# Two routing heads of each layer routed for both token tiles from one weight load, with the expert picks taken in twos

## What is computed

```python
q = einsum('bsd,de->bse', h, w_q).reshape(b, s, 8, 2, 128)
scores = einsum('bshid,hikd->bshik', q, sub_keys)      # 128 keys in each of two halves
top_s, top_i = top_k(scores, 16)
cand = top_s[..., 0, :, None] + top_s[..., 1, None, :] # 256 pairs
best_s, best_j = top_k(cand, 16)
experts = i1 * 128 + i2 ; gates = softmax(best_s)
act = gelu(einsum('td,tkd->tk', h, u_tab[experts]))
out = einsum('tk,tkd->td', gates * act, v_tab[experts])
```

## Time and profile before

| what | value |
|---|---|
| the runs shown, median | 1546.36 us |
| the profiled execution's own time | 1547.98 us |
| its span, first to last instruction | 1546.1 us |
| mean granted TensorE clock | 0.826 of full |
| PE busy (matmul) | 1049.1 us, 68% |
| VectorE (DVE) busy | 1083.2 us, 70% |
| ScalarE (ACT) busy | 575.1 us, 37% |
| GpSimd (POOL) busy | 619.7 us, 40% |
| moved by DMA | 623.55 MB, mean 403 GB/s |

### The profile page before, as it was taken

How to read it: one execution, slowest core, us unless ns; L and a number is a source line. 1 busy time by engine, 2 the same in 40 slices (tenths; PEclk the granted TensorE clock), 3 DMA queues, 4 the chain that set the end, 5 groups by cost and what they waited for, 6 DMA issues and landing times. The chain is left out here.

```text
span 1546.1 us, 19439 instructions
## 1 busy us (share of the span) xinstructions
PE 1049.1 (68%) x6790; PEld 532.8 (34%) x6790; DVE 1083.2 (70%) x2485; ACT 575.1 (37%) x1768; POOL 619.7 (40%) x571
## 2 busy tenths in 40 slices
PE   8898656785854668776775667788588465565555
PEld 6685312333531334332552334333255111111111
DVE  8777998646999685654789767564579965444444
ACT  5544433623444433441544431354234432221222
POOL 0034345442753533443343433444243354455441
PEclk9999877887986988787897788889698777667767
DMA  9289999999999999999999999999999999999997
GB/s 381 89 326 421 420 421 420 421 421 405 422 421 368 411 422 421 421 421 421 409 421 421 421 421 421 421 422 420 422 386 421 421 421 422 421 421 422 421 421 304
DMA packets 86642, 623.55 MB, mean 403 GB/s; under 512 B 10000, under 2 KB 10128, under 8 KB 11792
## 3 DMA queue, kind: packets, MB, share of 16 engines
q0 software_dynamic: 73728, 536.90, 83.7%
q1 hardware_dynamic: 12816, 85.41, 13.4%
HBM read 621.23 MB, written 1.05 MB: 402 GB/s over the span
## 5 line engine op out<-in xcount | busy, mean ns | idle before, releaser
L583 POOL DMA_INDIRECT slots<-experts,idx x512 | 593.2, 1159 | 886.5 <-PE psum L1830 709.9
L1427 DVE CUSTOM_DVE_ANT_0 slots<-slots,h 128x1024 f32<-128x1024 f32 x512 | 615.9, 1225 | 390.8 <-DMA slots<-experts,idx 387.6
L1830 PE MATMUL psum<-slots,diag 64*64 64x512 f32 x4088 | 599.3, 737 | 312.4 <-ACT diag L947 312.3
L1830 PEld LDWEIGHTS psum<-slots,diag 64*64 64x64 f32 x4088 | 175.8, 165 | 684.2 <-ACT diag L947 368.9
L931 ACT ACTIVATE ge<-ge 128x4 f32<-128x4 f32 x130 | 26.7, 205 | 437.3 <-DVE ge L1427 436.3
L1752 PE MATMUL psum<-hT,ring 128*128 128x128 f32 x992 | 131.3, 297 | 20.7 <-DMA ring<-weights 16.0
L931 ACT ACT_TABLE_LOAD x55 | 70.6, 1283 | 194.7 <-DVE ge L1427 194.3
L947 ACT ACTIVATE diag<-cst,ge 128x64 f32<-128x64 f32 x511 | 136.5, 336 | 6.7 <-PE psum L1830 2.5
L1752 PEld LDWEIGHTS psum<-hT,ring 128*128 128x128 f32 x992 | 127.7, 212 | 23.5 <-issue 17.7
L938 ACT ACTIVATE ge<-ge,gate 128x1 f32<-128x1 f32 x512 | 109.1, 283 | 4.2
L1525 PE MATMUL psum<-ring,hT 128*128 128x256 f32 x192 | 52.2, 433 | 17.5 <-DVE work L981 17.5
(11 more groups left out here) (292 smaller groups left out, 1075.4 us busy)
## 6 DMA issues: line engine op xcount, KB each, us to landing
ring<-weights SPq DMA_DIRECT2D x32, 1152.0 KB, 10.0
ring<-weights SPq DMA_DIRECT2D x26, 1024.0 KB, 9.2
slots<-weights SPq DMA_DIRECT2D x11, 1024.0 KB, 20.0
slots<-experts,idx POOLq DMA_INDIRECT x512, 20.8
ring<-weights SPq DMA_DIRECT2D x2, 1056.0 KB
sml<-small SPq DMA_DIRECT2D x2, 652.0 KB, 9.1
slots<-weights SPq DMA_DIRECT2D x1, 1056.0 KB, 9.0
xs<-x SPq DMA_DIRECT2D x2, 512.0 KB, 13.2
```

The costliest lines, as they stand in the source:

```text
L583: pool.indirect_dma_start(out=slot[:, place(E), :], out_offset=None, in_=src, in_offset=bass.IndirectOffsetOnAxis(ap=idx[:, n % 2, e:e + 1 ...
L1427: ins = dve.tensor_tensor_reduce(u, u, h2[:, n % 2, :], 1.0, 0.0, ALU.mult, ALU.add, d[:, i:i + 1])
L1830: ins = pe.matmul(acc[HALF * half:HALF * half + HALF, i, :], diag[rows, d % DIAGS, :], slot[rows, place(E), D + half * 512:D + half * 512 ...
```

## The change

It does five things.

1. **Shared heads.** Heads seven and eight (numbers 6 and 7, `SHARED`) of the two tiles of a layer are routed side by side: tile n's head 6, then tile n+1's head 6, then the same for head 7, n being the even step. The block of weights is loaded once (`owner`, `RING`) and given back after the second tile's use (`given_back`). The odd tile's transposed activations have their own place for that (`hR_`: `W[0]`).
2. **Groups of two picks.** GRP = 2, so 64 groups in a step.
3. **Rows in two densities.** In steps 0 and 2 the rows up to `h2T` of the next tile are spread over the first EARLY = 38 of 64 groups, and the ten routing rows (four of the pair, six of the next tile's own heads) over the other 26. In step 1, 22 mixing rows and six routing rows are spread over all 64. Routing heads are counted by their turn in the order (`turn_of`), not by 8n + h.
4. **`adds`.** Ahead of twelve kinds of rows (`FOLLOWS`) TensorE adds the group that is waiting before it starts on the row.
5. **The opening.** In `MIX0`, `qkv3` and `qkn0` come before `scan0`, the second subtraction of `scan0` becomes `scan_im` behind `qkn1`, `mul1` to `mul3` come later, tile 1's `p`, `qkv0` and `qkv1` come before `route1`. SP loads the first block of `qkv` before the constants.

The diff, cut to its core:

```diff
-GRP = 4
+GRP = 2
@@ rows
-       ... ("h2T", "rp"), ("route0",))
+       ... ("h2T",))
 MIX0
-        "power4", "qkv0", "f", "prep", "fx", "ln", "mul0", "mul1", "mul2", "mul3", "rotate0", "rotate1", "cum", "cm",
-        "qkv1", "rotate2", "bu", "qkv2", "scan0", "qkv3", "qkn0", "scan1", "qkn1", "qkv4", "pool", "qkT", "pre0", "pre1",
-        "mixp", "sq1", "scan2", "scan3", "scan4", "scan5", "scan6", "logits0", "scan7", "big0", "logits1", "scan8",
...
-        ("xT", 1), ("hTe", 1), "rp1", ("u", 1), "soft0", ("uT", 1), "route1", "soft1", ("p", 1), ("up", 1), ("f", 1),
+        "power4", "qkv0", "f", "prep", "fx", "ln", "mul0", "rotate0", "rotate1", "cum", "cm", "mul1", "mul2",
+        "qkv1", "rotate2", "bu", "qkv2", "qkv3", "qkn0", "scan0", "qkn1", "scan_im", "qkv4", "pool", "qkT", "pre0", "pre1",
+        "mixp", "mul3", "sq1", "scan1", "scan2", "scan3", "scan4", "scan5", "scan6", "logits0", "scan7", "big0", "logits1",
...
+        "route0", ("xT", 1), ("hTe", 1), "rp1", ("u", 1), "soft0", ("uT", 1), ("p", 1), ("up", 1), ("qkv0", 1),
+        ("f", 1), ("fx", 1), ("ln", 1), ("qkv1", 1), "route1", "rp2", "soft1", ("cum", 1), ("cm", 1), ("qkv2", 1), ...
+SHARED = (6, 7)
+OWN = tuple(h for h in range(PH) if h not in SHARED)
+EARLY = (TOPK * SHARED[0] - SLOTS - 7) // GRP
+FOLLOWS = {"normT", "u", "qkv0", "y", "glu", "qkT", "att1", "att2", "att3", "att4", "out0", "h2T"}
+def routing(heads):
+    rows = []
+    for (n, h), ahead in zip(heads, heads[1:] + [None]):
+        rows.append((n, (f"route{h}",) + ((("rp%d" % ahead[1], ahead[0]),) if ahead else ())))
+    return rows
+def rows_of(n):
+    if n == STEPS - 1:
+        return [], 0, QUADS
+    pair = [(n + i, h) for h in SHARED for i in range(2)]
+    if n == 0:
+        rows = [(1, r) for r in ((), ("qkn",), ("qkT", "v"))]
+        rows += routing([(0, h) for h in OWN[2:]]) + [(1, r) for r in MIX1]
+    else:
+        rows = [(n + 1, r) for r in MIX]
+    if n % TILES:
+        rows = last_row(rows, n + 1, OWN[0]) + routing([(n + 1, h) for h in OWN])
+        return rows, len(rows), QUADS
+    rows = last_row(rows, n, SHARED[0])
+    late = routing(pair + [(n + 1, h) for h in OWN])
+    ...
+    return rows + late, len(rows), EARLY
@@ script
-            while at < len(rows) * (quad + 1) // QUADS:
+            due = (early * (quad + 1) // until if quad < until else
+                   early + (len(rows) - early) * (quad + 1 - until) // (QUADS - until))
+            while at < due:
                 step, row = rows[at]
+                if FOLLOWS.intersection(row):
+                    order.append(("mix", "adds", n))
@@ ring
+def owner(n, i):
+    return (n - n % TILES, i) if i - CH_ROUTE in SHARED else (n, i)
-RING = [c for c in USES if not in_slot(*c)]
+RING = list(dict.fromkeys(owner(*c) for c in USES if not in_slot(*c)))
+def given_back(n, i):
+    return uses(n + 1, i) if i - CH_ROUTE in SHARED else uses(n, i)
-                    sp.wait_ge(S["chunk_used"], uses(*RING[c - 2]))
+                    sp.wait_ge(S["chunk_used"], given_back(*RING[c - 2]))
@@ SP, the opening
             chunk(CH_POOL)
+            chunk(CH_Q)
             sp.dma_start(cst[:, P:], consts[:, P:]).then_inc(S["cst_in"], 16)
...
-            for i in range(6):
+            for i in range(1, 6):
@@ the odd tile's activations
+        def hR_(n):
+            return W[0][:, :].rearrange("p (a b) -> p a b", a=KD) if n % TILES else hT
@@ VectorE, scan
                     link(tt(w3[0], w3[0], spare, ALU.add))
-                    link(tt(w3[1], w3[1], w3[3], ALU.subtract))
+                if part == 9:
+                    scan_im(n)
@@ TensorE
+            def adds(n):
+                add_last()
```

More of the change, by code:

```diff
@@ L103, with last_row @@
         ("att3", "max3", "nrm3"), ("att4", "attg", "sq"), ("merge", "out0"), ("out1", "x1a"),
[2 rows of a table removed]
-ROUTES = tuple((f"route{h}",) for h in range(1, PH))
+        ("out2", "x1p"), ("out3", "x1"), ("h2T",))
+SHARED = (6, 7)
[7 more added lines that the diff above has]
+    return rows
+def last_row(rows, n, h):
+    step, row = rows[-1]
+    return rows[:-1] + [(step, row + ((f"rp{h}", n),))]
+def rows_of(n):
[12 more added lines that the diff above has]
+    late = routing(pair + [(n + 1, h) for h in OWN])
+    if n == 0:
+        late = [(step, row + ((f"tab{5 + i - 4}", TILES),) if 4 <= i < 7 else row) for i, (step, row) in enumerate(late)]
+    return rows + late, len(rows), EARLY
 def script():
@@ L116, in script @@
     for n in range(STEPS):
-        if n == 0:
-            rows = [(1, r) for r in ((), ("qkn",), ("qkT", "v"))]
-            rows += [(0, r) for r in ROUTES[1:]] + [(1, r) for r in MIX1]
-        else:
-            rows = [(n + 1, r) for r in MIX + ROUTES] if n + 1 < STEPS else []
+        rows, early, until = rows_of(n)
         at = 0
@@ L128, in script @@
             done = at
-            while at < len(rows) * (quad + 1) // QUADS:
+            due = (early * (quad + 1) // until if quad < until else
+                   early + (len(rows) - early) * (quad + 1 - until) // (QUADS - until))
+            while at < due:
                 step, row = rows[at]
-                order += [("mix", s, 2 if s[:3] == "tab" else step) for s in row]
+                if FOLLOWS.intersection(row):
+                    order.append(("mix", "adds", n))
+                order += [("mix", s, step) if type(s) is str else ("mix",) + s for s in row]
                 at += 1
@@ L136, in script @@
                 order += [("mix", "soft" + s[5:], step) for s in row if s[:5] == "route"]
-    for quad in (QUADS, QUADS + 1):
-        order += [("open", n, quad), ("close", n, quad)]
-    return order + [("mix", "drain", STEPS - 1)]
+    return order + [("open", n, QUADS), ("close", n, QUADS), ("mix", "drain", STEPS - 1)]
 ORDER = script()
@@ L158, in chunk_order, with turn_of, routes_before @@
     return order
+def owner(n, i):
+    return (n - n % TILES, i) if i - CH_ROUTE in SHARED else (n, i)
 USES = chunk_order()
-RING = [c for c in USES if not in_slot(*c)]
+RING = list(dict.fromkeys(owner(*c) for c in USES if not in_slot(*c)))
+RSEQ = [(b, int(a[5:])) for kind, a, b in ORDER if kind == "mix" and a[:5] == "route"]
+def turn_of(n, h):
+    return RSEQ.index((n, h))
+def routes_before(stage):
+    return sum(1 for kind, a, b in ORDER[:ORDER.index(stage)] if kind == "mix" and a[:5] == "route")
+def given_back(n, i):
+    return uses(n + 1, i) if i - CH_ROUTE in SHARED else uses(n, i)
 FREE = CH_POOL
@@ L191, in experts_of @@
     start, end = PICKS * n + GRP * quad, PICKS * n + GRP * quad + GRP
-    if start >= PICKS * STEPS:
-        alone = PICKS * STEPS - 2 + quad - QUADS
-        return range(alone, alone + 1)
-    return range(start, min(end, PICKS * STEPS - 2))
+    last = PICKS * STEPS - 1
+    return range(start, min(end, last)) if start <= last else range(last, last + 1)
 BY_VECTOR = {PICKS * STEPS - 1}
@@ L1838, in close @@
                 waiting.append((n, quad))
-            run(dict(warm=warm, pre=pre, logits=logits0, turn=turn0, pv=pv0, normT=normT, xT=normT, u=u, p=p_, f=f_, oua=out_a, bu=bu, qkv=qkv, y=y_, glu=glu, qkT=qkT, att=att, pool=pool_,
+            run(dict(adds=adds, warm=warm, pre=pre, logits=logits0, turn=turn0, pv=pv0, normT=normT, xT=normT, u=u, p=p_, f=f_, oua=out_a, bu=bu, qkv=qkv, y=y_, glu=glu, qkT=qkT, att=att, pool=pool_,
                      mixp=mixp, merge=merge, out=out_b, h2T=h2T, rp=rp, route=route), lambda n, quad: None, close)
```

58 lines of the change are left out of this document (28 added, 30 removed), and 15 rows, old and new, of tables (MIX, MIX0, MIX1).

## The result

The change makes the kernel slower: 1570.25 us in the median of four runs (1568.42 to 1576.19) against 1545.98 us for the kernel before in runs beside them, a ratio of 1.0158 with a 95% interval of 1.0145 to 1.0171. The prediction was 1525.0 us, 1519 to 1536, with 94% on faster. It was wrong in sign.

The account below looks back on a forecast made before the run. The prediction took DMA bytes at 421 GB/s, plus holes when queues ran empty, as the bound. Its terms, -11.2 - 1.9 - 5.2 - 4.8 + 1.5 + 0.5 = -21.1 us, gave 1525 us as a median, range 1519 to 1536.

Parts of the forecast that it names:

- Part 1: Routing loads of heads 6 and 7: one load for two tiles, four loads or 4.72 MB fewer, -11.2 us.
- Part 2: The opening: the new order brings the first logits 1.97 us earlier, -1.9 us, bounds -2.0 to 0.
- Part 3, "`adds` puts the waiting group ahead of that wait": Around `x1`, `h2T` and `rp`: GpSimd's 20 us pauses fall apart into about 8 and 10 us, -4.8 us.
- Part 3, "With groups of two, two picks fewer wait, 5 us of transfer more in reserve": All steps: slots are held for two picks fewer, giving the DMA queue 5 us more transfer in reserve.
- the turn from step 0 to 1: Routing rows at the end of step 0: no group has two rows any more, -5.2 us, bounds -5.7 to 0.
- What is denser: Step 0's picks 12 to 38: VectorE falls 9.5 us behind, mostly covered by the reserve; +1.5 us, 0 to +7.
- step 2's mixing rows: 22 rows in 76 picks, 3.45 per row instead of 4.27; VectorE and TensorE stay under nine tenths busy: zero.
- More instructions: All steps: 126 more gelus, 26 us on ScalarE, covered by its wait for dots: zero.
- Part 4: The end: TensorE's shorter bursts may run the last picks at a lower clock, +0.5 us.
- signs of being wrong: A new dip around 150 to 230 or after 860 us, long TensorE waits for ring loads, or first gather at 86 us.
- sign of being right: GpSimd's longest pause on adds under 15 us; others included 28 loads and no 20 us stretch below about 400 GB/s.
- Rival C: Mixing rows of steps 0 and 2: the engines set the rows' pitch, 72 us longer, 1597 us; chance 0.03.

Follow-up runs that it names:

- experiment 7: The kernel of experiment 1 with the four shared blocks loaded once for each tile again, the order kept: 1547.96 us.
- experiment 11: The kernel before on groups of two, with TensorE keeping one more group waiting ahead of a group with a routing row, all 32 loads: 1546.96 us.
- experiment 1: The kernel after without `adds` ahead of any row, all else kept: 1539.77 us.
- experiment 8: The kernel after with `adds` left out ahead of the four attention steps and `out0`, kept elsewhere: 1545.31 us.
- experiment 9: The kernel after with `adds` placed behind its row's own steps instead of ahead of them: 1541.4 us.
- experiment 6: The kernel of experiment 1 with TensorE keeping one more group waiting ahead of a group with a routing row, added behind the row: 1534.04 us.
- experiment 4: The kernel before on groups of two, with its own order and all 32 loads: 1550.52 us.
- experiment 2: The kernel after on groups of four instead of two, `adds` kept: 1554.66 us.

## Why the prediction was wrong

- **Part 1 (the loads, -11.2 us)** was right in mechanism and bytes. 28 loads and 80.69 MB are there. The price is 8.2 us where the late rows have holes (experiment 7). With most of those closed it wasn't measured alone: the 12.9 us of experiment 11 hold the rest of the order as well.
- **Part 2 (the opening, -1.9 us)** was mis-sized. The multiply did move the logits, whose maximum starts at 45.98 us instead of 48.01. But the prediction said that VectorE is the engine that others wait for up to about 62 us and gave the whole advance to the first indices. Of the advance 1.59 us were left at the operation of the first two lines, before and after. Then a new wait of 1.16 us for TensorE, which the kernel before didn't have, took 1.13 us of it; the wait of 2.72 us for ScalarE stood there before as well. The first gather of the kernel after starts at 85.81 us, 0.45 us earlier than in the earlier trace rows:

```profile
62.11 1.28 DVE L978 SCALAR_TENSOR_TENSOR xs<-psum,rn,xs 128x1024 f32<-128x1024 f32 x1
60.52 1.28 DVE L1038 SCALAR_TENSOR_TENSOR xs<-psum,rn,xs 128x1024 f32<-128x1024 f32 x1
62.97 0.74 DVE L1235 SCALAR_TENSOR_TENSOR ring<-uT,sml,psum 128x128 f32<-128x128 f32 x2 [1.16 <-PE psum L1604]
66.43 0.43 DVE L1038 SCALAR_TENSOR_TENSOR work<-ring 128x256 f32<-128x256 f32 x1 [2.72 <-ACT ring L802]
```

```profile
85.81 1.12 POOL L644 DMA_INDIRECT slots<-experts,idx  x1 [68.26 <-DVE idx L1038]
```

- **Part 3, "`adds` puts the waiting group ahead of that wait" (-4.8 us), is the step that failed.** It costed an operation that is put ahead of another by the one place where that helps (ahead of `h2T`, where TensorE stood idle), and not by the eleven other rows where it is written. There TensorE's order is: sums, then what VectorE waits for; and the sums need weights that ScalarE has not made yet. The prediction never asked who is queued behind the sums. Experiments 1, 8 and 9 give it 30.5 us, 24.9 of them in five rows, and all but 1.6 (1541.4 - 1539.77, within the spread of the runs) by its place ahead of the row.
- **Part 3, "With groups of two, two picks fewer wait, 5 us of transfer more in reserve",** left out that VectorE's cover for a wait is the dots of a group, four of 1.225 us before, two now. In the late routing rows each row asks for scores that stand behind new sums: no such wait with fours, 21 waits with twos (experiment 1), of 1.7 us in the mean and up to 3.0. The prediction's 14.6 us of VectorE for such a row, against 15.2 of DMA, is 16.3 with the mean wait and 17.6 with the longest. So the turn from step 0 to 1 (-5.2 us) did not come: 480 to 500 us lost 3.0 us and 500 to 520 lost 1.9. Experiment 6 removes the wait, and with it the holes from 400 to 520 us. The gain of the smaller group itself is real in the changed order (23.2 us without `adds`) and absent in the old one (experiment 4).
- **The sum itself** hid an interaction. `adds` costs 30.5 us with twos and gains 8.3 us with fours (1562.92 without, 1554.66 with), 38.7 us between the two. By the holes, the attention rows lose alike in both; with fours the late rows have no wait of their own and `adds` repairs long pauses, with twos it takes away the reserve that the late rows need. That last link is read from the places of the holes (experiments 1, 2, 8), not tested by itself.
- **"What is denser" (+1.5 us)** was near for twos: 200 to 220 us lost 3.3 us with `adds` and nothing without. That is partly luck. The prediction has VectorE fall 2.5 us behind in these rows before the change; its own sum, redone for 40 picks, gives 102.5 us of VectorE against 110.8 of DMA, so no lag, and the step to 9.5 us behind was larger than it took it to be. With fours the same stretch lost 7.1 and 11.6 us (200 to 240). The attention rows of step 0 have no term at all in the prediction, and lost 12.6 us. For step 2's mixing rows it wrote zero because both engines would be under nine tenths busy; they lost about 1 us with twos (880 to 1140 us), but 5.9 us with fours and `adds` and 15.9 with fours alone. Busy shares say nothing of a ring in which each engine waits for the next.
- **A pause not costed.** The tables on GpSimd stood at the routing rows before and cost nothing; now the queue is short there. Their part is 2.1 us without `adds`, within the noise; with it the hole there is 10.6 us, of which their part wasn't measured.
- **More instructions (zero)** held nearly. There are 127 gelus more, 25 us of ScalarE. Twos on the old order cost 0.2%, 3.7 us (experiment 4), but the routing matmul first takes 3.6 of them away again with no instruction fewer (experiment 11).
- **Part 4 (the end, +0.5 us)** did not come: from the start of the last dot to the end of the span it is 7.4 us in both profiled executions (1538.72 to 1546.1, 1560.95 to 1568.4).
- **The signs.** Three of the signs of being wrong came: a stretch far below 400 GB/s, a new dip in step 0's dense rows (200 to 220 us), and a first gather at 86 us. One sign of being right came too, GpSimd's longest pause on the sums under 15 us (10.6), and misled: that 15 us cost nothing was read where the queue is full.

Rival C was nearest in kind: rows paced by the chain of the engines. It was to decide from half a microsecond too long per row on; in the attention rows it was 3.9 us (13.84 against 9.96). But it made the chain too long by the density of the rows, and with twos it is `adds` that does: in experiment 9 the same rows, as dense, came every 9.36 us. It was given 3% and 1597 us, since it was priced over all rows, and argued away by VectorE's idle time between 870 and 1110 us in the kernel before, whose order had no `adds`.

## What to carry to other kernels

Before an operation is moved ahead of another in an in-order queue, write down three names: what it waits for, who is queued behind it, and who waits for that one. It may stand ahead only where its input is ready before the next one's. And when a group is made smaller, count what cover it gives each wait and not only the buffers it frees: a wait for scores that four dots hid showed 21 times under two, up to 3 us long.

The version that beats both is that of experiment 6: the shared loads and groups of two, no `adds`, and one more group of sums held back before a routing row, 1534.04 us, 0.8% less than the kernel before (ratio 0.9916 [0.9900, 0.9933]).

## What the runs showed of the hardware

- **TensorE's clock makes the wait worse.** In the kernel after the sums that follow an idle of 3.61 us ran in part at the lower clock: 32 matmuls in 6.42 us, and the stretch has a granted clock of 0.82. In experiment 9, with shorter idles between, the same stretch had a clock of 1.00, and 16 took 1.95 us, so 3.9 for 32. Of the 13.84 us of a row some 2.5 are this. The Trainium skill, page "TensorE: Matmul & The Clock Gate", section What's actually happening, has the clock fall to 1.2 GHz for an array that idles; the trace agrees: 16 matmuls took 3.69 us after an idle of 15.33 us (experiment 1) and 1.95 us after one of 1.73 us (experiment 9), which is nearly the ratio of the two levels.
- **VectorE and GpSimd are slow at the same time.** While GpSimd made tables in the kernel after, VectorE's dots took 1.29 to 1.47 us where their mean is 1.226, and pairs of 128x128 operations of GpSimd took 2.61 to 2.83 us, whereas pairs of twice that width took 1.19 to 1.39 us some 12 us later, with the same line, and pairs of 128x128 took 0.77 to 1.64 us in the kernel before. One of VectorE's index operations, 0.17 us in the median of 31, took 3.09 us at 403.58 us, beside the wide pairs. That they hinder each other is the likely reading and wasn't tested alone. Two of the dots, and the index operation:

```profile
385.50 1.29 DVE L1491 CUSTOM_DVE_ANT_0 slots<-slots,h 128x1024 f32<-128x1024 f32 x1
...
392.10 1.47 DVE L1491 CUSTOM_DVE_ANT_0 slots<-slots,h 128x1024 f32<-128x1024 f32 x1
...
403.58 3.09 DVE L1456 SCALAR_TENSOR_TENSOR idx<-ex 128x16 uint32<-128x16 f32 x1
```

One of the wide pairs, and one of the 128x128 pairs of the kernel before:

```profile
402.92 1.20 POOL L606 TENSOR_TENSOR work<-rot 128x256 f32<-128x256 f32 x2
...
412.72 0.87 POOL L545 TENSOR_TENSOR rot<-rot,work 128x128 f32<-128x128 f32 x2
```
